# Two chunks between scores and turn, a third for the norm roots, and output halves that wait tile by tile

## What is computed

```python
x = x + concat(attention_1, attention_2) @ w_out      # h = rms_norm(x) @ w_in feeds both
x = x + square(relu(rms_norm(x) @ w_up)) @ w_down
# A, B and D normalise q and k of every head:
q = q * rsqrt(mean(q * q) + eps) * gain
# A, B, D:
probs = softmax(q @ k.T + bias_or_mask); out = probs @ v
# C:
weight = where(s < t, exp(log_sigmoid(z) + suffix_sum(log_sigmoid(-z))), 0)
# D: the bias is a table by relative position, with -1e30 where chunks of 64 frames may not see each other
```

## Time and profile before

| | |
|---|---|
| median of 3 executions | 2612.36 us (2610.92 to 2613.93) |
| profiled execution | 2609.5 us |
| its span, first to last instruction | 2607.7 us |
| TensorE matmul busy | 2548.9 us, 98% of the span |
| VectorE, ScalarE, GpSimd busy | 1437.3, 980.9, 191.4 us |
| mean granted TensorE clock | 0.995 |
| stage A, beside the input projection of B | from about 133 us |
| stage B, beside the output projection | from about 345 us |
| stage C, beside the input projection of D | from about 1450 us |
| stage D, beside the output projection | from about 1654 us |

### The profile page before, as it was taken

One profiled execution on the slowest core, in us unless ns is written; L12 is line 12 of the kernel. 1 busy time (PEld: TensorE's weight loads), 2 busy tenths in 40 slices (PEclk: granted clock), 3 DMA queues, 4 the chain that ended last, 5 costly groups with the idle time before them and its releaser, 6 DMA issues.

```text
span 2607.7 us, 46987 instructions
## 1 busy us (share of the span) xinstructions
PE 2548.9 (98%) x19241; PEld 2504.6 (96%) x19241; DVE 1437.3 (55%) x1628; ACT 980.9 (38%) x1223; POOL 191.4 (7%) x189
## 2 busy tenths in 40 slices
PE   7999989999999999999999999999999999999998
PEld 7989889999999999999999998899999999999998
DVE  6577856754454454455644554667544544544543
ACT  4333444433333333333333443444333333333332
POOL 2011222200000000001300001222000000000000
PEclk9999999999999999999999999999999999999999
DMA  5545545444454544454555545544444454444453
GB/s 208 165 163 169 179 167 173 161 167 168 164 168 164 168 164 169 163 170 162 170 192 169 174 156 190 176 170 162 168 165 169 164 169 163 169 163 168 165 181 128
DMA packets 119059, 439.48 MB, mean 169 GB/s; under 512 B 14467, under 2 KB 14861, under 8 KB 116565
## 3 DMA queue, kind: packets, MB, share of 16 engines
q1 hardware_dynamic: 109440, 398.77, 45.1%
q0 software_dynamic: 6416, 31.46, 3.3%
q10 hardware_dynamic: 3012, 6.46, 0.7%
HBM read 426.37 MB, written 10.19 MB: 167 GB/s over the span
## 4 chain that ended last, share of the span: by engine, by line
PE 92%; DVE 4%; issue 1%; ACT 1%; DMA 1%; POOL 0%; SPq 0%; ACTq 0%; DVEq 0%; POOLq 0%
PE ps L382 27%; PE ps L384 27%; PE ps L383 27%; PE ps L348 3%; PE ps L350 2%; PE ps L349 2%; DVE w_low L1127 1%; ACT w_high L802 1%; PE ps L559 1%; PE ps L511 0%; DMA resid<-in_x 0%; POOL scr L1657 0%; DVE scr L1369 0%; DVE top L1367 0%; DMA scr<-norm_rows 0%
## 5 line engine op out<-in xcount | busy, mean ns | idle before, releaser
L1127 DVE TENSOR_TENSOR w_low<-raw,w_high 128x1024 fp32r<-128x1024 f32 x756 | 953.9, 1262 | 946.4 <-ACT w_high L802 943.9
L802 ACT CAST w_high<-raw 128x1024 fp32r<-128x1024 f32 x756 | 793.3, 1049 | 1459.5 <-PE ps L384 1358.3
L382 PE MATMUL ps<-x_parts,w_high 128*128 128x288 f32 x3472 | 1039.1, 299 | 20.3 <-DVE x_parts L1201 14.2
L383 PE MATMUL ps<-x_parts,w_high 128*128 128x288 f32 x3472 | 1025.2, 295 | 0.0
L384 PE MATMUL ps<-x_parts,w_low 128*128 128x288 f32 x3472 | 1023.7, 295 | 0.0
L382 PEld LDWEIGHTS ps<-x_parts,w_high 128*128 128x128 f32 x3472 | 654.1, 188 | 28.5 <-issue 17.9
L383 PEld LDWEIGHTS ps<-x_parts,w_high 128*128 128x128 f32 x3472 | 659.0, 190 | 2.1 <-issue 1.9
L384 PEld LDWEIGHTS ps<-x_parts,w_low 128*128 128x128 f32 x3472 | 658.1, 190 | 0.0
L382 PE MATMUL ps<-hid_parts_a,w_high 128*128 128x288 f32 x1024 | 303.1, 296 | 0.0
L384 PE MATMUL ps<-hid_high_b,w_low 128*128 128x288 f32 x1024 | 302.3, 295 | 0.0
L383 PE MATMUL ps<-hid_low_b,w_high 128*128 128x288 f32 x1024 | 302.3, 295 | 0.0
(11 more groups left out here) (335 smaller groups left out, 1831.7 us busy)
## 6 DMA issues: line engine op xcount, KB each, us to landing
raw<-in_w SPq DMA_DIRECT2D x756, 512.0 KB, 3.2
tmp<-norm_rows ACTq DMA_DIRECT2D x6, 576.0 KB, 4.4
resid<-in_x SPq DMA_DIRECT2D x4, 576.0 KB, 7.9
out_y<-resid POOLq DMA_DIRECT2D x8, 288.0 KB, 2.5
scr<-in_k_past_B POOLq DMA_DIRECT2D x2, 1024.0 KB, 5.8
scr<-in_v_past_B POOLq DMA_DIRECT2D x2, 1024.0 KB, 6.5
scr<-in_k_past_C POOLq DMA_DIRECT2D x2, 1024.0 KB, 6.9
scr<-in_v_past_C POOLq DMA_DIRECT2D x2, 1024.0 KB, 7.8
```

What stands on the lines that cost most here:

```text
L382: pe.matmul(out, wh, high, start=k == 0, stop=end and apart)
L383: pe.matmul(out_low, wh, low, start=k == 0 and apart, stop=False)
L802: act.copy(w_high[:, kk % 2, :], raw[:, kk, :]).then_inc(high_ready, 1)
L1127: dve.tensor_tensor(w_low[:, kk % 2, :], raw[:, kk, :], w_high[:, kk % 2, :].bitcast(F32), ALU.subtract)\
```

## The change

Line numbers of the changed kernel are 9 to 14 lower in the later parts of the file. It does this:

- the turn moves from distance 1 to 2 for heads 0 to 7 of A, B and D, and for jobs 8 and 9 of C; what follows it (`pt_copy`, `values`, `mixed_high`, `mixed_low`) moves one window with it; jobs 8 and 9 of A, B and D keep their distances and start one window later in B and D; C starts one window later, its job 9 two;
- the multiply after the norm sums moves from distance 2 to 3, and the sums of most quads move by one to two windows;
- in B and D the spread roots of quads 2 and 3 go into free tiles of `proj` instead of `scr`, quad 3 in one transfer instead of two, and the squares of quad 3 wait for the sums of quad 2 instead of its multiply;
- `out_half` waits before its first chunk for all but the last of the results, and before its second chunk for the last;
- D's mask is put into the bias on the host; 8 mask additions on GpSimd and the mask's load fall away;
- the two turns of v in A move from windows 10 and 11 to 16 and 17, behind the sums of the forget gates, and the waits that guard bank 6 are swapped accordingly.

```diff
 START = {
     "A": [23 + n for n in range(H)] + [43, 45],
-    "B": [1 + n for n in range(H)] + [9, 11],
-    "C": [1 + 3 * n for n in range(H)] + [25, 27],
-    "D": [1 + n for n in range(H)] + [9, 11],
+    "B": [1 + n for n in range(H)] + [10, 12],
+    "C": [2 + 3 * n for n in range(H)] + [26, 29],
+    "D": [1 + n for n in range(H)] + [10, 12],
 }
...
-    "A": [("A", 0, 5), ("A", 1, 7), ("A", 2, 9), ("B", 0, 33), ("B", 1, 35), ("B", 2, 40)],
-    "B": [("B", 3, 0)],
-    "C": [("D", 0, 36), ("D", 1, 38), ("D", 2, 41)],
-    "D": [("D", 3, 0)],
+    "A": [("A", 0, 5), ("A", 1, 8), ("A", 2, 11), ("B", 0, 33), ("B", 1, 36), ("B", 2, 41)],
+    "B": [("B", 3, 1)],
+    "C": [("D", 0, 36), ("D", 1, 39), ("D", 2, 42)],
+    "D": [("D", 3, 1)],
...
-W_DOTS_S, W_FOLD, W_DOTS, W_V_A, W_PICK, W_LF = 2, 4, 4, 10, 12, 13
+W_DOTS_S, W_FOLD, W_DOTS, W_V_A, W_PICK, W_LF = 2, 4, 4, 16, 12, 13
...
+        def spread_quad(ph, g):
+
+            return spread_rows if ph == "A" or g < 2 else proj[:, 12:16, :] if g == 2 else proj[:, 8:12, :]
...
                 for i in range(HALF_CH):
                     c = base * CH + (OUT_G * half + j) * HALF_CH + i
+                    if j == 0:
+
+                        pe.wait_ge(hid_low_ready, before - 1 + i)
                     pe.wait_ge(low_ready, c + 1)
...
             def out_half(base, lead, half, before, window=None, windows=0):
 
-                pe.wait_ge(hid_low_ready, before)
                 for j in range(OUT_G):
-                    out_pair(base, lead, half, j, window)
+                    out_pair(base, lead, half, j, before, window)
...
-                for n in jobs_at(ph, w, 2):
+                for n in jobs_at(ph, w, 3, 2):
                     values(ph, n)
-                for n in jobs_at(ph, w, 1):
+                for n in jobs_at(ph, w, 2, 1):
                     turn(ph, n)
...
             def window_c(w):
                 prelude("C", w)
-                for n in jobs_at("C", w, 3):
+                for n in jobs_at("C", w, 4):
                     if n >= H:
                         turn_mixed("C", n)
-                for n in jobs_at("C", w, 3, 2):
+                for n in jobs_at("C", w, 3):
                     values("C", n)
-                for n in jobs_at("C", w, 2, 1):
+                for n in jobs_at("C", w, 2):
...
-                if ph == "A" and n == H:
-                    act.wait_ge(sem("B_normed"), 6)
                 act.wait_ge(sem(ph + "_turned"), n + 1)
...
-                for n in jobs_at(ph, w, 1):
+                for n in jobs_at(ph, w, 2, 1):
                     pt_copy(ph, n)
...
             def prelude(stage, w):
-                for ph, g in quads_at(stage, w, 2):
+                for ph, g in quads_at(stage, w, 3):
...
-                    if ph == "A" or n < H:
-                        dve.wait_ge(sem(ph + "_addend"), n + 1)
+                    if ph == "A":
+                        dve.wait_ge(sem("A_addend"), n + 1)
                     else:
                         dve.wait_ge(sem(f"{ph}_bias{n % 2}"), 16 * (n // 2 + 1))
...
-                for n in jobs_at(ph, w, 2, 3 if ph in "BD" else 2):
+                for n in jobs_at(ph, w, 3, 3 if ph in "BD" else 2):
                     mixed_low(ph, n)
...
-                    if ph in "BD" and i >= 6:
-                        pool.wait_ge(sem(ph + "_normed"), 6)
-                    elif i >= 2 and not (ph in "BD" and i >= 4):
+                    if i >= 2 and not (ph in "BD" and i in (4, 5)):
                         pool.wait_ge(sem(ph + "_sums"), i // 2)
...
-            masked("D", 0)
-            masked("D", 1)
             squares("D", 6, 8)
...
+        near = rows[:, REL0 + s.T[:, 0:TP] - t.T[0:TP]]
+        if ph == "D":
+            near = _np.where(chunked[None, 0:TP, 0:TP] < 0, neg, near)
```

More of the change, by code:

```diff
@@ L233, in build @@
         spread_rows = tmp[:, 0:4 * T].rearrange("p (f t) -> p f t", f=4)
-        spread_q0 = scr[:, 0:4 * T].rearrange("p (f t) -> p f t", f=4)
-        spread_q1 = [scr[:, at:at + 2 * T].rearrange("p (f t) -> p f t", f=2) for at in (3328, 9728)]
         def spread_pair(ph, i):
-            if ph in "BD" and i >= 6:
-                return spread_q1[i - 6]
-            whole = spread_q0 if ph in "BD" and i >= 4 else spread_rows
-            return whole[:, 2 * (i % 2):2 * (i % 2) + 2, :]
+            return spread_quad(ph, i // 2)[:, 2 * (i % 2):2 * (i % 2) + 2, :]
+        def spread_quad(ph, g):
+            return spread_rows if ph == "A" or g < 2 else proj[:, 12:16, :] if g == 2 else proj[:, 8:12, :]
         def spread_count(ph, g):
-            at = QUADS.index((ph, g))
-            return 16 * sum(2 if q[0] in "BD" and q[1] == 3 else 1 for q in QUADS[0:at + 1])
+            return 16 * (QUADS.index((ph, g)) + 1)
         sqs_dq = [scr[:, 2 * T * i:2 * T * (i + 1)].rearrange("p (f t) -> p f t", f=2) for i in range(2)]
@@ L332, in HID, with out_pair @@
                 return hid(True, k)[:, 0, :], hid(False, k)[:, 0, :]
-            def out_pair(base, lead, half, j, window=None):
+            def out_pair(base, lead, half, j, before, window=None):
                 e = base + lead + OUT_G * half + j
@@ L463, in turn_v @@
                 if ph == "A":
[L465 removed]
+                    pe.wait_ge(sem("B_cum_copied"), 1)
                     b = 6 + h
@@ L873, in spread_norm @@
                     act.wait_ge(sem(ph + "_normed"), 2 * g)
-                if ph in "BD" and g == 3:
-                    for i in range(2):
-                        act.dma_start(spread_q1[i], norm_rows[at:at + 1, 2 * i:2 * i + 2, :].to_broadcast([P, 2, T]))\
-                           .then_inc(sem("norm_spread"), 16)
-                else:
-                    whole = spread_q0 if ph in "BD" and g == 2 else spread_rows
-                    act.dma_start(whole[:, 0:n, :], norm_rows[at:at + 1, 0:n, :].to_broadcast([P, n, T]))\
-                       .then_inc(sem("norm_spread"), 16)
+                act.dma_start(spread_quad(ph, g)[:, 0:n, :], norm_rows[at:at + 1, 0:n, :].to_broadcast([P, n, T]))\
+                   .then_inc(sem("norm_spread"), 16)
             def copy_v(ph, h):
@@ L1041, in window_c @@
                 prelude("C", w)
-                for n in jobs_at("C", w, 3):
+                for n in jobs_at("C", w, 3, 4):
                     mixed_high("C", n)
-                for n in jobs_at("C", w, 1):
+                for n in jobs_at("C", w, 2):
                     if n >= H:
                         copy_weights(n)
-                for n in jobs_at("C", w, 2):
+                for n in jobs_at("C", w, 3):
                     if n >= H:
@@ L1695, in masked @@
                         pool.wait_ge(sem("A_sel_s"), 1)
-                elif ph == "B":
+                else:
                     if n == 0:
@@ L1699, in masked @@
                     m = mask_b if n < H else mask_bs
-                else:
-                    if n == 0:
-                        pool.wait_ge(sem("D_mask"), 16)
-                    m = mask_d
                 if ph == "B":
@@ L1720, in addends_beside @@
                     bias(ph, n)
-                    if n > 2:
+                    if n > 2 and ph == "B":
                         masked(ph, n - 1)
-                masked(ph, H - 1)
+                if ph == "B":
+                    masked(ph, H - 1)
                 bias(ph, H)
@@ L1806, in _ @@
             pool.wait_ge(hid_low_ready, hid_at["D"])
-            pool.dma_start(mask_d, ins["mask_d"][:, 0:WIDE]).then_inc(sem("D_mask"), 16)
             load_quad("D", 0)
@@ L1928 @@
     for ph, rows in (("A", a["t5_bias"][bucket].T), ("D", a["d_rel_bias"][0][clip].T)):
-        arrays["bias_" + ph] = rows[:, REL0 + s.T[:, 0:TP] - t.T[0:TP]].reshape(H, 2, P, TP)[:, ::-1]\
+        near = rows[:, REL0 + s.T[:, 0:TP] - t.T[0:TP]]
+        if ph == "D":
+            near = _np.where(chunked[None, 0:TP, 0:TP] < 0, neg, near)
+        arrays["bias_" + ph] = near.reshape(H, 2, P, TP)[:, ::-1]\
             .transpose(0, 2, 1, 3).reshape(H, P, 2 * TP)[:, :, 0:WIDE]
```

7 lines of the change are left out of this document (2 added, 5 removed).

## The result

The changed kernel took 2594.7 us (median of 4 executions, 2592.44 to 2594.92), the kernel before on the same chip 2611.6 (2609.76 to 2613.93): a ratio of 0.9933, with a 95% interval of 0.9916 to 0.9950. It is faster by more than the 0.2% that a measurement can tell. The forecast was 2596.5, in a range of 2589 to 2605. The profiled span fell from 2607.7 to 2591.5 us, 16.2 us less; the sum of the terms had been 15.9.

A forecast was written before the change was run, and what follows sets the result against it. TensorE was taken to bound the kernel, with some 35 us of waits and half clock within reach. Terms summing to 15.9 us, taken from the 2612.4 us median, gave 2596.5 us, range 2589 to 2605.

The forecast's parts named there:

- Part 1: A, B, D, turn one window later: first turns' waits go, new residual waits come; +0.65, +4.1, +0.7 us.
- In the steady windows they neither gain nor lose: Later head windows: residual ends at 376.46, TensorE asks at 377.12, so no gain or loss.
- Part 2: Squares and sums in A and B: +2.7 us; smaller terms of +0.6, +1.0 and +0.2 beside it.
- A's sample turn: Window 42: mask additions collide less with the next subtraction; +0.6 us of the turn's 1.6 us wait.
- D's quad 3: Its sums waited 1.0 us and get one window more: +1.0 us.
- Part 3: Stage C: later start +1.6 us; sample jobs wait 1.8 us each instead of 3.5, no half clock, +7.8.
- Part 4: Before the sums of D's quad 2: an uncovered chain makes a 7.2 us wait, half clock costs 2.5; net -4.8 us.
- Part 5: The rest: the first output chunk's 1.3 us wait for A's last residual goes, +1.35 us; other edits 0.
- A's early windows: Windows 5 to 16 of A: one multiply moves behind VectorE's full stretch, two turns of v move too; +0.2 us.
- (a): Rival: clock also falls behind new short waits in B, D, A's sums, C's two jobs, 1.7 us each; 2604; chance 0.15.
- (b): Rival: VectorE catches up, so the new residual waits (4.5 us) do not come; gain 20.4, 2592 us; chance 0.17.
- (c): Rival: each of 21 later heads waits 1.0 to 1.2 us for its residual; 2621 us, slower; chance in full 0.04.

The follow-up runs named there:

- the probe: The changed kernel with 36 TensorE waits of mixed length, on GpSimd memsets, put into the first feed-forward stage: 2697.5 us.
- the last kernel: The changed kernel with B's and D's key stores behind quad 2's squares and VectorE's quad 3 multiplies behind logits and residual in window 4: 2583.6 us.

## Why the prediction was right

Against the two profiled executions, term by term:

- *Part 1.* A: 1.35 gained, and no wait for a residual came (0.7 forecast). B: 1.74 + 2.97 went, 2.17 came, and half clock for 3.4 us stood behind both, so 2.5 instead of 4.1. The length of the wait was right (2.3), but that it would leave the clock alone was not: the sum counts 1.7 us as gained that were not. The waits of up to 1.6 us on which this was built say nothing of 2.2; behind waits of 2.0 to 2.6 us the clock fell in 15 of 26 cases. D: 1.55 + 0.76 (the prediction has 0.67) against 1.62, 0.7 as forecast. The cause named, multiplies ahead of the residual, is shown for 1.46 us of B's 2.17 by the run with the multiplies last; the lag of 1.5 us that the working has beside them is not shown, and in A, which has only the lag, no wait came. Nor does the gain belong to the turn's distance alone: the run with just that gained nothing.
- *"In the steady windows they neither gain nor lose"* was slightly wrong on the good side. The 5.12 us taken as the pace of before was that of every second window in B. With 4.85 us instead of 5.12 and 5.10 in two windows some 0.5 us were gained there, and in D 0.2.
- *Part 2.* 3.00 + 0.77 became 0.26 + 0.87 + 0.43, a gain of 2.2 (2.7 forecast). The wait forecast at 1.4 us came as a short wait for the squares and one for a subtraction slowed beside them. A's sample turn 0.6 and D's quad 3 1.0, both as forecast.
- *Part 3.* 1.6 for the start; for the jobs 3.47 + 3.36 and 4.4 of lost clock became 0.29 + 1.20 + 0.19 + 1.30, a gain of 8.3 (7.8). Each job was to pay 0.4 us at the turn and 1.4 at the subtraction behind it; it paid 0.2 to 0.3 and 1.2 to 1.3. The run of C alone shows this term by itself.
- *Part 4.* 7.08 us (7.2) and 2.7 of clock (2.5): -4.8, as forecast. The run with the store behind the squares shows that the whole wait hangs on the store's place in the queue, the run with quad 1 a window earlier that the lost window is worth 3.8 us of it. The share of the clock is less firm: behind the same wait of 7.08 us in four other profiles TensorE was busy at half clock for 2.97, 3.99, 5.20 and 6.16 us, so 1.5 to 3.1 us were lost.
- *Part 5.* 1.35 gained. The term was right for this kernel but not for the edit: the split also hides 5.2 us that the later sample jobs would have cost. The prediction priced the output wait by what it removes and did not ask what its absence would cost the rest. D's mask in the bias and the single transfer of quad 3's roots were put at 0; no run undoes either alone.

1.35 + 2.5 + 0.7 + 2.2 + 0.6 + 1.0 + 1.6 + 8.3 - 4.8 + 1.35 = 14.8, A's early windows 0.1 on the other side, so some 1.5 us of 16.2 are left over. By stage: from the first matmul of its first chunk to that of its 17th, stage B took 75.8 us instead of 79.4 (3.6 less, of which 2.5 are named), and stage D 73.9 instead of 75.8 (1.9 less, 1.7 named); between the two, where C lies, the terms account for all of it (5.0 less, 5.1 named). What is left over is therefore about 1.0 us in B, of which the shorter windows are half, 0.2 in D and 0.6 ahead of B, less 0.3 by which the first matmul came later. No run shows the cause of any of it.

That the sum came out within 0.3 us of the profiled gain is in part luck: B's clock (-1.7) was made good by terms that were set too low and by gains that nobody had forecast. The prediction's own list of what would prove it wrong had 0.50 of the clock behind waits under 3 us, and at 366 us that is what happened. So of the rivals, (a) came true in one of the five places it named, (b) in A only, and (c) not at all.

## What to carry to other kernels

When a step is moved by a window, list every in-order queue whose next entry waits for it: here a store that nothing nearby waited for stood between a multiply and the squares of something else, and cost 9.8 us in the profile (7.08 of wait, 2.7 of clock) and 9.1 us by the medians, beside a gain of 16.2. In the kernel before it had cost 3.25 and 1.7 already. A distance that is longer by one helps only where what follows it has the same slack: the turn's distance alone gained nothing. And a guard that shows no wait in the profile, like the one ahead of the output half, may be what the next edit runs into; price an edit with the others undone, too.

## What the runs showed of the hardware

The clock fell behind none of the 37 waits of TensorE of 0.7 to 1.84 us counted above. Behind waits of 2.0 to 3.5 us it fell 18 times in 19 in the probe and 19 times in 34 elsewhere, and each of the five times behind 7.08 us. The Trainium skill, "TensorE: Matmul & The Clock Gate", section "Why this matters for your kernels", warns of idle gaps of more than about 3 us between bursts of matmuls. The trace agrees behind 7.08 us; below that the measurements, which decide, differ from it both ways, with 15 of 26 waits of 2.0 to 2.6 us followed by 1.2 GHz and waits of 3.25 and 3.43 us that were not.

The clock also fell where TensorE had had no wait over 0.6 us for 60 us and none at all for the last 5: in five of the fourteen profiled executions, at about 200 us, in the forget gates' run of small matmuls (window 14 of A), four times for 3.41 us and once for 6.82. From the last kernel's clock view:

```profile
199.66:206.48 6.82, 6.82 (x48) 4.78 (x46) 1.70 (x2) 0.00 (x0) 2.25 (x4) 0.50 0.61 210
```

In the changed kernel the same place ran at 1.00. Such stretches, and up to 3 us more or less in the first 320 us, come and go with nothing edited there. I take them, with the stretches behind waits of 2 to 3 us, to be why kernels that differ by 2 us in their waits can't be told apart by their medians; no run shows that.
